# VectorE's order in two attention loops: the bias sum and maximum of a pair stand two pairs ahead, before the output scaling

## The reference

```python
# layer 0, neighbourhood attention: 16 heads of width 64
s_win = einsum(q_r, k_r) + bias                  # latent keys of a window, with a learned bias
s_ctx = einsum(q_r, kc)                          # 256 context keys
p = softmax(concatenate([s_win, s_ctx]))         # context queries: softmax over context keys alone
o = einsum(p_win, v_r) + einsum(p_ctx, vc)
# layer 1, window attention: 16 query heads, 4 key heads, rotary positions, a sink logit per head
s_win = where(valid, einsum(qb, kb), -1e30)
p = softmax(concatenate([s_win, s_ctx, s_sink]))
o = einsum(p_win, vb) + einsum(p_ctx, vc)
```

## Time and profile before

| what | value |
| --- | --- |
| median of 3 runs | 3303.24 us (3296.48 to 3305.59) |
| the profiled execution, its own time | 3270.63 us |
| its span | 3268.9 us |
| mean granted TensorE clock | 0.985 of full |
| TensorE busy | 3143.2 us (96%) |
| VectorE busy | 1937.8 us (59%) |
| ScalarE busy | 1577.0 us (48%) |

### The profile page before, as it was taken

The page is one execution under the profiler, slowest core; times in us unless marked ns, Lnnn a source line. Parts: engine busy times, 40 slices in busy tenths (PEclk is TensorE's granted clock), DMA queues, the critical chain, the costliest instruction groups (busy, mean ns, idle before and its releaser), DMA issues.

```text
span 3268.9 us, 63095 instructions
## 1 busy us (share of the span) xinstructions
PE 3143.2 (96%) x26594; PEld 3012.7 (92%) x26594; DVE 1937.8 (59%) x3076; ACT 1577.0 (48%) x2707; POOL 395.5 (12%) x482
## 2 busy tenths in 40 slices
PE   8999999999999999999999998889999999998998
PEld 7889998899999899999999996889999999996998
DVE  5965569645554555667357734484467635776554
ACT  5654455644444444455245545453355524555544
POOL 0000040000000000122001511160011400130000
PEclk9999999999999999999999999899999999999999
DMA  6334473367777777555345541243455424550352
GB/s 240 120 116 168 171 256 109 117 254 295 299 288 279 274 306 254 195 190 189 102 158 194 198 161 33 84 145 138 151 188 196 173 97 154 193 193 16 117 198 99
DMA packets 102866, 580.81 MB, mean 178 GB/s; under 512 B 16977, under 2 KB 25297, under 8 KB 49658
## 3 DMA queue, kind: packets, MB, share of 16 engines
q1 hardware_dynamic: 86176, 489.54, 41.8%
q0 software_dynamic: 13568, 84.91, 6.9%
q10 hardware_dynamic: 2842, 2.34, 0.2%
HBM read 575.08 MB, written 11.04 MB: 179 GB/s over the span
## 4 chain that ended last, share of the span: by engine, by line
PE 79%; DVE 10%; ACT 4%; DMA 3%; issue 2%; POOL 2%; ACTq 0%; POOLq 0%; SPq 0%; DVEq 0%
PE PS L936 71%; DVE CONV L2053 3%; DMA TMP<-in_w_mod 2%; DVE WL L1724 2%; PE PS L1218 2%; PE PS L977 2%; POOL TMP L867 1%; ACT WH L1333 1%; PE PS L1205 1%; PE PS L1098 1%; PE PS L1191 1%; PE PS L1092 1%; ACT SB L1566 0%; DVE TMP L1824 0%; DVE RSTD L1743 0%
## 5 line engine op out<-in xcount | busy, mean ns | idle before, releaser
L1724 DVE TENSOR_TENSOR WL<-RAW,WH 128x1024 fp32r<-128x1024 f32 (+1 forms) x1018 | 1156.2, 1139 | 888.9 <-ACT WH L1333 882.0
L936 PE MATMUL PS<-UH,WH 128*128 128x256 f32 (+1 forms) x5536 | 1530.8, 283 | 25.4 <-DVE TMP L2113 7.8
L936 PE MATMUL PS<-UL,WH 128*128 128x256 f32 (+1 forms) x5536 | 1516.3, 280 | 0.0
L936 PE MATMUL PS<-UH,WL 128*128 128x256 f32 (+1 forms) x5536 | 1516.1, 280 | 0.0
L1333 ACT ACTIVATE WH<-RAW 128x1024 fp32r<-128x1024 f32 (+1 forms) x1018 | 983.0, 968 | 866.0 <-PE PS L936 837.3
L936 PEld LDWEIGHTS PS<-UH,WH 128*128 128x128 f32 x5536 | 1035.5, 190 | 42.5 <-issue 18.6
L936 PEld LDWEIGHTS PS<-UL,WH 128*128 128x128 f32 x5536 | 1033.9, 190 | 0.6
L936 PEld LDWEIGHTS PS<-UH,WL 128*128 128x128 f32 x5536 | 1033.7, 189 | 0.0
L936 PE MATMUL PS<-HIDH,WH 128*128 128x256 f32 (+1 forms) x2112 | 545.9, 279 | 0.0
L936 PE MATMUL PS<-HIDL,WH 128*128 128x256 f32 (+1 forms) x2112 | 544.0, 278 | 0.0
L936 PE MATMUL PS<-HIDH,WL 128*128 128x256 f32 (+1 forms) x2112 | 543.8, 278 | 0.0
(11 more groups left out here) (207 smaller groups left out, 2297.5 us busy)
## 6 DMA issues: line engine op xcount, KB each, us to landing
RAW<-in_w_gu SPq DMA_DIRECT2D x255, 1024.0 KB, 4.8
RAW<-in_w_dn SPq DMA_DIRECT2D x168, 704.0 KB, 4.1
MRAW<-in_w_mod POOLq DMA_DIRECT2D x36, 1024.0 KB, 6.9
TMP<-in_w_mod POOLq DMA_DIRECT2D x36, 1024.0 KB, 9.8
RAW<-in_w_in SPq DMA_DIRECT2D x30, 1024.0 KB, 8.1
RAW<-in_w_na SPq DMA_DIRECT2D x20, 1024.0 KB, 4.8
RAW<-in_w_o SPq DMA_DIRECT2D x12, 1024.0 KB, 4.8
RAW<-in_w_proj SPq DMA_DIRECT2D x8, 1024.0 KB, 4.8
```

What stands on the lines that cost most here:

```text
L936: last = pe.matmul(ps[:, a:b], w, m[:, a:b], start=first and a == 0, stop=final and b == n)
L1724: dve.tensor_tensor(WL[slot][:, 0:hi - lo], RAW[:, p.raw(s), lo:hi], WH[slot][:, 0:hi - lo].bitcast(F32), ALU.subtract).then_inc(s_lo, 1)
```

## The change

In VectorE's loop of `attention` the call of `biased` moves by one pair and behind the reciprocal: `biased(1)` now stands ahead of the loop, and the loop's body is inverted(g), biased(g+2), scaled(g-1), where it was biased(g+1), inverted(g), scaled(g-1). It acts on both attentions of the second block. Seen from the scaling of g-1, the sum and maximum of g+2 stood behind it (in the next turn of the loop) and now stand ahead of it. No instruction is added or left out.

```diff
                 biased(0)
+                biased(1)
                 for g in range(a.total + 3):
-                    if g + 1 < a.total:
-                        biased(g + 1)
                     if g < a.total:
                         inverted(g)
+                    if g + 2 < a.total:
+                        biased(g + 2)
                     if 1 <= g <= a.total:
                         scaled(g - 1)
```

## The result

The changed kernel took 3254.88 us, the median of 12 runs (3245.72 to 3272.83); the kernel before, over its 12 runs by then, 3291.97 us (3276.46 to 3306.1). The ratio is 0.9913, with a 95% interval from 0.9888 to 0.9937: 29 us faster, by 21 to 37. (The two medians lie 37 us apart, because the 12 times of the changed kernel fall into two groups, five from 3266 to 3273 us and seven from 3246 to 3256; the ratio rests on all of them.) The forecast said faster, 3280 us, with a range from 3267 to 3298. The direction was right; the time is 12 us under the range. The gain forecast, 22.9 us or a ratio of 0.9930, lies inside the measured interval.

The account below looks back on a forecast made before the run. TensorE, busy 96% of the span, stood 20.4 us in two attentions where exponentials wait for VectorE's maxima. Neighbourhood 12.5, window 5.2 and clock 5.2 make 22.9 us; 3270.63 becomes 3247.7, scaled to the runs' median 3280, range 3267 to 3298.

Parts of the forecast that it names:

- Sum and maximum earlier: Neighbourhood attention: VectorE starts the sum when scores end, closing TensorE's 1.47 us gap; that attention's gain taken as 12.5 us.
- The second gap: Neighbourhood attention: TensorE's 0.47 us gap per period behind the copy of turned probabilities closes too, by 0.15 us.
- Window attention: Second attention: TensorE's 0.57 us gaps per head pair and 1.64 at the end go; 5.2 us gained, bounds 3.4 to 5.7.
- The 1.4 us ahead of the first turned output: Window attention: TensorE's 1.40 us gap there stays, since it waits for the rotation of queries.
- The clock: Behind the last long neighbourhood gap: TensorE's fall to 1.2 GHz goes; 5.2 us gained, bounds 0 to 5.2.
- The sum: Whole kernel: 12.5 + 5.2 + 5.2 = 22.9 us gained, a ratio of 0.9930.
- The absolute time: Whole kernel: the shown runs' median, 3303.24 us, scaled by 0.9930 gives 3280.
- Scaling later: Both attentions: scaling behind sum and maximum costs nothing, up to 0.5 us late within 2.1 us of TensorE cover.
- the slower rival (4): Both attentions: late sum and maximum delay the scaling that the next value product awaits; 13 us slower, 3316; chance 3%.
- (1): Neighbourhood attention: gaps go but the clock's fall stays or comes elsewhere; 17.7 us gained, 3285; chance 22%.
- (2): Both attentions: TensorE comes to wait for ScalarE instead; only 8.6 us gained, 3294; chance 8%.
- (3): Attentions: nothing moves, as exponentials wait for something other than the maximum, such as GpSimd's bias; 3303; chance 5%.

Follow-up runs that it names:

- na_only: Kernel before with the new VectorE order in the neighbourhood attention alone; ratio to the kernel before 0.9933, attentions 109.3 and 82.0 us.
- before_3: Kernel before, unedited, one more profiled execution; neighbourhood attention 125.7 us, window attention 86.4 us.
- before_4: Kernel before, unedited, another profiled execution; neighbourhood attention 131.1 us, window attention 84.8 us.
- delay2: Changed kernel plus two idle maxima ahead of the scaling, behind each latent pair's maximum in the neighbourhood attention; ratio to the kernel before 1.0076.
- old_filled: Kernel before plus nine idle TensorE transposes in the 1.47 us gap of each neighbourhood head pair; ratio to the kernel before 0.9971.
- old_tail: Changed kernel with the neighbourhood attention's last head pair back in the old order; ratio to the kernel before 0.9934, that attention 116.0 us.
- delay1: Changed kernel plus one idle maximum ahead of the scaling, behind each latent pair's maximum in the neighbourhood attention; ratio to the kernel before 0.9930.
- after_3: Changed kernel, unedited, one more profiled execution; neighbourhood attention 108.4 us, window attention 74.1 us.

## Why the prediction was right in its mechanism and short in its time

- **Sum and maximum earlier: right.** The stand of TensorE in the neighbourhood attention fell from 17.7 us (mean of the five old ones) to 6.0 (four new ones): 11.8 us, forecast 12.5. The period is 12.77, where 12.75 was TensorE's own. The second gap closed to within 0.1 us and not wholly: my margin of 0.15 us left out what lies between the end of the copy and the start of the turning, itself 0.15 (2033.29 to 2033.44 in the earlier trace rows), so there was none.
- **Window attention: right, its clock missed.** The same sums of gaps give 10.6 us before (the four of the kernel before and na_only: 11.3, 10.9, 10.4, 9.6, 11.1) and 5.3 after: 5.3 of standing gone, 5.2 forecast. (My lower bound of 3.4 counted six gaps of 0.57; the trace has four, 2.3 us.) But the attention got 8.4 us shorter (83.5 to 75.1), so 3 us are the clock's, for which I had counted nothing. This part is the least certain: the 3 us come mainly from the long late falls of before_3 and before_4, and delay2 had such a fall under the new order; with all profiles of each order (6 and 8) 7.4 us are gained and 2 of them are the clock's. The 1.4 us ahead of the first turned output stayed, as did the start.
- **The clock: the step that failed.** I took 5.2 us, the price of the one fall that the first profile had. The loop's periodic gaps bring falls in every execution of the old order, in a number that differs: half-clock time of 10.9, 24.3, 10.3, 22.1 and 27.8 us, 19.1 on average, against 1.1 in the new order. Half of the 18 us is lost time: 9 us. The attentions agree: 129.8 less 108.9 is 20.9, and 20.9 less 11.8 of standing leaves 9.1. With the window attention's 3 it is 12 us where the sum had 5.2 and called that the upper bound; the clocks of the timed runs say 9.6 (6.7 to 12.5). "Gaps of 1.47 us in the periods before had no fall behind them" was true of that execution only; old_filled shows that filling these very gaps keeps the clock up, and old_tail that one gap of 1.9 can be followed by a fall. The rule of the Trainium skill that I weighed ("TensorE: Matmul & The Clock Gate", Part 1: the moment of a change differs from run to run) agrees with these traces. I used it in one direction only, to take the term away; here the number of falls differs as well, and the execution that I read had fewer than most.
- **The sum.** Standing 11.8 + 5.3 and clock 9.1 + 3.1 make 29.3 us, ratio 0.9911; the runs gave 0.9913 and 0.9915. With the 9.6 of the timed runs' clocks it is 26.7 us, inside the measured interval too. How the gain splits is known to 2 or 3 us.
- **The absolute time.** I scaled from 3303.24, the median of three runs. Over 12 runs it was 3291.97, 11 us lower; the clock's 7 us come on top. 3280 less 18 is 3262; the two medians of the changed kernel, 3254.88 and 3267.31, lie on both sides. It took both misses to leave the range: 3291.97 less the 22.9 forecast is 3269, and 3303.24 with the true gain is about 3274, both inside it. The larger share is the base's, a plain matter of three runs. I had widened the terms' bounds (3279 to 3289) by the 9 us over which these three spread; the 12 runs spread over 30 (3276 to 3306). The two misses went the same way by chance.
- **Scaling later: cost nothing, as said, but with less room.** I gave 2.1 us of cover and called 0.5 us of it used. In delay2's timeline the cover is 1.6 us behind the first latent product, beside which a context pair is turned, and 2.1 behind the second; in the changed kernel the second scaling starts 0.5 us behind its product. delay1 shows that the rest is under 1.2 us, since the second latent pair inherits the lateness of the first. The wait that the slower rival (4) named is real: it makes delay2 25 us slower than before, though there more work holds the scaling up and not, as in the rival, a sum that starts late. That took 2.4 us more work ahead of each latent scaling; with 1.2 us more the kernel was still faster than before.
- **Other rivals.** (1) The fall inside the loop did not stay: the four new-order profiles of the first table have none from the 20th us of the neighbourhood attention to its last 2 us. The fall around the start of the projection stayed. (2) ScalarE did not become the bound: what is left of the second gap, which it ends, is under 0.1 us a period. (3) The exponentials did wait for the maxima: that wait fell from 41.5 to 10.6 us, and the bias sum waits for scores alone, never for GpSimd. The rest of the span does not take the gain back: old order 3059.6 to 3095.1 (mean 3078.9 over four), new order 3075.2 to 3088.7 (3082.8 over three).

## What to carry to other kernels

In an in-order engine, put what frees another engine two steps on ahead of what waits for a result of this step, and check how much later the second may come before somebody waits for it. A periodic gap of 1.5 us in TensorE's work can cost nearly as much again through the clock (here 9.1 us beside 11.8 of standing), and by a different number of falls in each execution: read the clock from several executions before giving it a price. Compare stages between two profiles and not spans: here the spans said 3268.9 against 3271.1, and the stage 127.3 against 108.3.

## What the runs showed of the hardware

The dense stages run at one of two paces with the granted clock at 1.00 in both. The products of line 936 in the same 200 us, before and after (windows of that line on TensorE alone):

```profile
1500.00:1700.00 200.00, 200.00 (x1767) 1.00 0.42 146
```

```profile
1500.00:1700.00 200.00, 200.00 (x1700) 1.00 0.40 139
```

That is 113 against 118 ns a product, 4%, constant over a stage of 270 us and different from stage to stage. In this stretch the first profile of before, after_3 and na_only run at 113, the other three profiles of before and the other two of the changed kernel at 118: it belongs to the execution, not to the kernel. In before_3 some 5,300 products more run at the slower pace than in the first profile of before; by 4.45 ns each (117.78 less 113.33, start to start) that is 24 of the 35.5 us by which their rests differ. It is also why the first two profiles showed no gain: that of the changed kernel has some 5,700 more at the slower pace, 25 of the 29.1 us by which its rest is longer (3088.7 against 3059.6). What sets it stays open; no run here was made to find out.
